# A further pass woven into the expert's own products, in two mixture-of-experts layers on one Trainium2 core

## What is computed

```python
idx = top2 of the best group's scores          # 768 assignments over 16 experts
gates = scores at idx, normalised
for e in range(16):                            # per layer; w1, w3, w2 are 1024 x 1024
    y[e] = (silu(x[e] @ w1[e]) * (x[e] @ w3[e])) @ w2[e]     # x[e]: the tokens of e
out[token] = sum over its two experts of gate * y[e][token]
x = x + g2 * out
```

## Time and profile before

| | us |
|---|---|
| median of 3 runs | 1597.15 (1591.28 to 1598.04) |
| the profiled execution | 1596.13 |
| its span | 1593.1 |
| PE busy in the span | 1482.3 (93%) |
| DVE, ACT busy | 632.8 (40%), 298.3 (19%) |
| read from HBM | 493.06 MB, 310 GB/s over the span |

### The profile page before, as it was taken

How to read it: one execution, slowest core, us unless ns; L and a number is a source line. 1 busy time by engine, 2 the same in 40 slices (tenths; PEclk the granted TensorE clock), 3 DMA queues, 4 the chain that set the end, 5 groups by cost and what they waited for, 6 DMA issues and landing times.

```text
span 1593.1 us, 21276 instructions
## 1 busy us (share of the span) xinstructions
PE 1482.3 (93%) x7798; PEld 719.7 (45%) x7799; DVE 632.8 (40%) x1845; ACT 298.3 (19%) x503; POOL 0.2 (0%) x4
## 2 busy tenths in 40 slices
PE   6999999988899999989999799897999999999996
PEld 3545555645344344434344355454344444344433
DVE  4534666343224332322333548834222333432333
ACT  4422222131010010011010347522101011011001
POOL 0000000000000000000000000000000000000000
PEclk9999999998999999999999899998999999999999
DMA  9448776762969999999987501525699999999992
GB/s 342 178 142 306 262 255 249 313 283 77 391 250 397 425 427 427 425 427 427 424 368 278 196 1 53 211 106 211 285 417 429 424 428 427 403 427 427 424 392 101
DMA packets 67711, 495.29 MB, mean 311 GB/s; under 512 B 4608, under 2 KB 21264, under 8 KB 28368
## 3 DMA queue, kind: packets, MB, share of 16 engines
q1 hardware_dynamic: 66048, 489.33, 75.3%
q10 hardware_dynamic: 1616, 5.33, 1.0%
HBM read 493.06 MB, written 1.58 MB: 310 GB/s over the span
## 4 chain that ended last, share of the span: by engine, by line
PE 78%; DMA 11%; DVE 5%; ACT 3%; issue 2%; ACTq 0%; DVEq 0%; SPq 0%
PE PS L833 76%; DMA halves<-in_moe_w 11%; PE PS L837 2%; DVE xc L1837 1%; ACT hT L575 0%; DVE halves L1658 0%; DVE misc L1658 0%; DVE halves L1651 0%; DVE halves L1649 0%; ACT hT L816 0%; DVE halves L1477 0%; DVE halves L1650 0%; ACT halves L635 0%; ACT halves L736 0%; ACT h L636 0%
## 5 line engine op out<-in xcount | busy, mean ns | idle before, releaser
L833 PE MATMUL PS<-halves,hT 128*64 128x512 f32 x3072 | 674.0, 598 | 17.3 <-DMA halves<-in_moe_w 14.8
L833 PEld LDWEIGHTS PS<-halves,hT 128*64 128x64 f32 x3072 | 218.7, 138 | 454.7 <-issue 429.9
L833 PE MATMUL PS<-hT,halves 128*128 128x384 f32 x640 | 219.7, 499 | 8.4 <-ACT halves L702 6.5
L833 PE MATMUL PS<-halves 128*32 128x512 f32 (+5 forms) x928 | 193.7, 508 | 1.4 <-ACT halves L538 0.7
L833 PEld LDWEIGHTS PS<-hT,halves 128*128 128x128 f32 x640 | 122.2, 194 | 108.0 <-issue 24.3
L1918 DVE COPY misc<-PS 64x512 f32<-64x512 f32 x32 | 21.9, 683 | 335.6 <-PE PS L833 335.6
L833 PEld LDWEIGHTS PS<-halves 128*128 128x128 f32 (+2 forms) x928 | 96.6, 158 | 83.8 <-issue 43.3
L1837 DVE SCALAR_TENSOR_TENSOR xc<-PS,MOD,xc 128x128 f32<-128x128 f32 x336 | 112.3, 409 | 13.8 <-PE PS L833 11.8
L833 PE MATMUL PS<-stack,h 128*128 128x128 f32 x768 | 100.4, 292 | 12.6 <-issue 5.4
L833 PEld LDWEIGHTS PS<-stack,h 128*128 128x128 f32 x768 | 96.0, 206 | 24.0 <-issue 19.8
L597 ACT ACTIVATE hT<-PS 128x512 f32<-128x512 f32 x32 | 19.1, 598 | 433.1 <-PE PS L833 433.1
(11 more groups left out here) (234 smaller groups left out, 978.3 us busy)
## 6 DMA issues: line engine op xcount, KB each, us to landing
halves<-in_moe_w SPq DMA_DIRECT2D x192, 2048.0 KB, 18.2
halves<-in_ada_w SPq DMA_DIRECT2D x48, 1024.0 KB, 6.6
halves<-in_hy_w_in SPq DMA_DIRECT2D x12, 1024.0 KB, 5.1
halves<-in_rg_w_in SPq DMA_DIRECT2D x4, 2048.0 KB, 19.2
halves<-in_hy_w_out SPq DMA_DIRECT2D x4, 1024.0 KB, 9.3
halves<-in_rg_w_out SPq DMA_DIRECT2D x2, 2048.0 KB, 10.5
halves<-in_rg_wa SPq DMA_DIRECT2D x1, 2048.0 KB, 8.4
halves<-in_rg_wx SPq DMA_DIRECT2D x1, 2048.0 KB, 10.9
```

The lines of the kernel that those rows point to most:

```text
L833: return nc.tensor.matmul(out, lhsT, rhs, start=start, stop=stop)
```

## The change

- PE's `extra_pass` is cut into six functions. An expert with `extra > 0` takes a branch of its own in which the first further pass is woven with the base pass: gather, hidden units turned, the pass's tokens turned, w1 and w3 of the pass, **the base w2**, the pass's units turned, (odd experts: both halves of the next tokens), the pass's w2, (odd: the gates), combines. Second and later passes keep an inner loop inside that branch. An expert with `extra < 1` takes a second branch with the old order. The shared parts (units turned, spread, tokens, gates, base w2) so stand twice in the program.
- For an even expert of the branch with a pass, the whole `spread` of the pair before now stands ahead of the pass, and `pass_gather` waits until all eight of its tiles are added (`added(l, group, 8)`, before `8 * r`).
- DVE adds the pass's tiles after it has copied the base output (`pass_added`), and the next expert's base products wait for the pass's tiles in banks 2 and 3. The combine banks are in another order, Xyo and the units' transposition use banks 1 and 7.
- SP: `load_last` now also waits for the pass's w2 (`x_w2_mm`); `freed` waits for `w1_mm` and `w13_mm` of the last user and for its passes, in place of `w13_last`, which is gone.
- PE and DVE read the last expert's counts once more after the loop, and wait for its pass before the layer's last combines.

```diff
-MOE_RELEASE = ("w13_last", "w13_last", "w13_last", "w13_last", "w2_first", "w2_mm")
+MOE_RELEASE = ("w1_mm", "w1_mm", "w13_mm", "w13_mm", "w2_first", "w2_mm")
+X_RELEASE = ("x_w1_mm", "x_w1_mm", "x_w13_mm", "x_w13_mm", "x_w2_mm", "x_w2_mm")
...
                 def load_last(r, e):
+                    passes = passes_to(e - 1)
                     for c in range(4, 6):
-                        load_expert(c, r, e, (MOE_RELEASE[c], NE * l + e))
+                        load_expert(c, r, e, (MOE_RELEASE[c], NE * l + e), (X_RELEASE[c], X_BEGUN + passes))
...
                         for b, at, done_sem in ((2, 0, "w1_mm"), (3, 2, "w13_mm")):
+                            passed(done, b)
                             for k in range(KD):
...
-                        with pe.If(extra > 0):
-                            with pe.Fori(0, extra) as j:
-                                extra_pass(r, group, e, done + j)
...
+                        with pe.If(extra > 0):
+                            if not r:
+                                with pe.If(group > 0):
+                                    spread(l, group, done, 0, 4)
+                                    pe.wait_ge(S("hid"), before("hid", l) + e + 1)
+                                    spread(l, group, done, 4, KD)
+                            pass_gather(r, group, e, done)
+                            units_turned()
+                            pass_tokens(done)
+                            pass_first_two(r, done)
+                            second_matrix()
+                            pass_units(done)
+                            if r:
+                                with pe.If(group < NE // UNROLL - 1):
+                                    pe.wait_ge(S("pick"), before("pick", l) + e + 3)
+                                    tokens_of_two(0)
+                                    tokens_of_two(1)
+                            pass_last(r, done)
+                            if r:
+                                gates_turned()
+                                pe.wait_ge(S("gpT"), before("gpT", l) + group + 1)
+                            pe.wait_ge(S("yo"), GATED + before("yo", l) + e + 1)
+                            pass_combine(done)
+                            with pe.If(extra > 1):
+                                with pe.Fori(1, extra) as j:
+                                    pass_gather(r, group, e, done + j)
...
+                        with pe.If(extra < 1):
...
+                            units_turned()
...
+                            second_matrix()
...
+                extra = pe.value_load(counts_i[0:1, NE - 1:NE], min_val=0, max_val=NX)
+                done = pe.value_load(counts_i[0:1, 2 * NE - 1:2 * NE], min_val=0, max_val=2 * LAYERS * NX)
+                pe.wait_ge(S("x_acc"), X_ADDED + 8 * (done + extra))
...
+                        with dve.If(extra > 0):
+                            pass_added(group, done)
```

More of the change, by code:

```diff
@@ L163, in added, with last_user, freed @@
     return ADDED - 8 + before("acc_done", l) + 8 * pair + tiles
-def freed(l, slot):
-    c = slot % 6
-    return MOE_RELEASE[c], NE * l + (NE - 1 if slot < 4 else NE)
+def last_user(slot):
+    return NE - 2 if slot < 4 else NE - 1
+def freed(l, slot, passes):
+    c, e = slot % 6, last_user(slot)
+    return (MOE_RELEASE[c], NE * l + e + 1), (X_RELEASE[c], X_BEGUN + passes[e])
 ADDED, SPREAD, GATED, X_ADDED, X_BEGUN = 16, 8, 1, 9, 1
@@ L597, in expert_layer, with units_turned, next_tokens @@
                         a.activation(hid, PS[:, 2, :], ACT.Sigmoid).then_inc(S("sig"), 1)
[L598 to L614, removed]
+                        def units_turned():
+                            act.wait_ge(S("hidT_mm"), before("hidT_mm", l) + e + 1)
+                            a.activation(hidT, PS[:, 2, :].rearrange("p (c m) -> p c m", m=P), ACT.Copy) \
+                                .then_inc(S("hidT"), 1)
+                        def next_tokens():
                             with act.If(group < NE // UNROLL - 1):
@@ L1290, in expert_layer @@
                             last.then_inc(S("gpT_mm"), 1)
-                        else:
-                            with pe.If(group > 0):
-                                spread(l, group, done + extra, 4, KD)
-                        passed(done + extra, 6)
-                        pe.wait_ge(S("acc_done"), added(l, group, SPREAD_BANKS.index(6) + 1))
-                        pe.wait_ge(S("hidT"), before("hidT", l) + e + 1)
-                        for k in range(KD):
-                            half = k // 4
-                            if k % 4 == 0:
-                                arrived(4 + half, r, group)
-                            for g in range(2):
-                                last = mm(PS[m * g:m * g + m, 6, :], hidT[:, k % 4, m * half:m * half + m],
-                                          weight(r, 4 + half)[:, k % 4, HALF * g:HALF * g + HALF], k == 0, k == KD - 1)
-                            if k == 3:
-                                last.then_inc(S(MOE_RELEASE[4]), 1)
@@ L1307, in expert_layer, with second_matrix @@
[L1307 to L1312 removed]
+                        def second_matrix():
+                            passed(done, 6)
+                            pe.wait_ge(S("acc_done"), added(l, group, SPREAD_BANKS.index(6) + 1))
+                            pe.wait_ge(S("hidT"), before("hidT", l) + e + 1)
+                            for k in range(KD):
+                                half = k // 4
+                                if k % 4 == 0:
+                                    arrived(4 + half, r, group)
+                                for g in range(2):
+                                    last = mm(PS[m * g:m * g + m, 6, :], hidT[:, k % 4, m * half:m * half + m],
+                                              weight(r, 4 + half)[:, k % 4, HALF * g:HALF * g + HALF], k == 0, k == KD - 1)
+                                if k == 3:
+                                    last.then_inc(S(MOE_RELEASE[4]), 1)
+                            last.then_inc(S("w2_mm"), 1)
```

162 lines of the change are left out of this document (103 added, 59 removed).

## The result

The changed kernel takes **1695.45 us** (median of 4 runs, 1691.29 to 1700.51), the kernel before 1596.27 us: a ratio of 1.0627, 95% interval 1.0605 to 1.0648. The forecast was 1602 us, with a range up to 1668. It is 6.3% slower, and the range missed it. The profiled execution's span is 1695.2 us, 102.1 more than before.

The account below looks back on a forecast made before the run. PE and weight transfers were taken to bound the expert layers in turns. From 1596.1 us, -6.3 (layer 0 weaving), +2.8, +7.0 and +2.0 (missing code blocks, expert 7's gain included) gave 1601.6, median 1602; range 1584 to 1668.

Parts of the forecast that it names:

- The weaving, pass by pass: Five expert passes: new durations from interleaving with base work, worth -6.3 us in layer 0 and -1.5 in layer 1.
- The transfer chain's net gain of 1.0: Layer 0, experts 0 and 2: 8.0 us gained, less jump idle and slow clock, against 3.6 lost to later slots.
- The code's place: PE's expert loop: a pair without a pass touches eight instruction blocks in layer 0, nine in layer 1.
- each number having its place: PE's instruction store: block numbers have fixed places, so 32 and 40 collide, one miss per pair in layer 1.
- C: Rival, chance 0.25: first block in is given up first, nine miss every pair in layer 1; 1647 to 1683 us.
- A missing block costs 1.9 to 3.6 us: PE's jumps to blocks not held: each stop costs this much, read from the earlier trace.
- In layer 0 only expert 14's way back misses: Layer 0, after expert 13's pass: the only missing block there, +1.9 to 3.6 us, taken as +2.8.
- Later misses, under 5.1 per pair, hide behind the transfers: Layer 1 after its first pairs: misses cost nothing, except the one at expert 15, +2.0 us.
- A: The forecast itself, chance 0.33: eight blocks kept in fixed places, about two packets per layer 1 pair, 1602 us.
- B: Rival, chance 0.25: more than eight blocks stay, none is lost, no packets in layer 1; median 1590 us.
- E: Rival, chance 0.10: the weaving itself disappoints, expert 2's later slots costing more than expert 0 saves; 1604 to 1612 us.
- D: Rival, chance 0.07: only neighbouring instruction blocks are kept, so layer 0 suffers as well; about 1725 us.

Follow-up runs that it names:

- straight code, held: Changed kernel without loops for second and later passes, loop head at slot 64 of a block and backward jump announced, 1586.96 us, 0.9954 of the kernel before.
- late-return run: Woven order with TensorE's code written once, head at slot 64, next layer's slots returned at the old time: 1595.71 us, 0.9994 of the kernel before.
- aligned kernel of point 3: Changed kernel without loops for second and later passes, loop head at slot 64 of a block, no announcement: 1596.76 us, 1.0012 of the kernel before.
- old order padded: Kernel before with dead code in each pass branch, giving its loop the changed kernel's block layout: 1697.04 us, 1.0641 times the kernel before.
- kernel without later loops: Changed kernel without its loops for second and later further passes on all three engines, no alignment: 1668.27 us, 1.0487 times the kernel before.

## Why the prediction was wrong

**The weaving, pass by pass: right in its durations.** Forecast and measured (straight code, held): expert 0, 24.4 and 24.7 us (387.82 to 412.50); expert 2, 30.7 and 30.9 (459.29 to 490.22); its first transfer after 13.4 and 13.3 (472.61); expert 13, 30.0 and 30.7; expert 15 to the last combines, 29.6 and 29.4. The transfer chain's net gain of 1.0 (0.8 by its own terms: 8.0 less 1.9 and 1.7 is 4.4, not 4.6) came out as a loss of 0.3, near enough. Costed at nothing and rightly so: the earlier return, by the late-return run. So the order inside each pass was forecast well. The sum was not: -6.3 in layer 0 and -1.5 in layer 1 stand against some -3 in all, because layer 1 as a whole gave +1.7 although expert 7's pass gave its 1.4 (44.6 instead of 46.0 us). In the changed kernel all of it drowned.

**The code's place: right.** The count said eight blocks per ordinary pair in layer 0 and nine in layer 1, and the trace shows exactly this border: none in layer 0's settled pairs, packets in layer 1's, and the sides change when the code moves by 0.19 block. The one exception is layer 0 in the profile of the aligned kernel of point 3, with two packets at eight blocks.

**The failing step** is the sentence that took "eight are kept, each number having its place, so that 32 and 40 push each other out, one miss per pair". By fixed places a pair would fetch two blocks in the old order padded and four in the kernel without later loops; both fetched about nine, as when each block that comes pushes out one that is needed soon. The forecast gave this order, C, a quarter, and its price of a pair (61.3 to 66.4 us) met the 64.9 us of the kernel without later loops. The only argument for a fixed place was that it was "nearest to the rows", but no row told one order from the other: both keep eight, and the old kernel never needed a ninth. This was a choice between 1602 and 1665 with nothing in the trace behind it. Layer 1 was put at +9.0, the pass's gain counted in, and cost 68.2 us in all.

**A second step was mis-sized**: "A missing block costs 1.9 to 3.6 us", from the earlier trace rows. Where no work is queued it was 5.4 us beside transfers, and the smaller stops are best read as what queued products left uncovered. With it fell "In layer 0 only expert 14's way back misses", at +2.8: the way out of the pass of expert 13 misses three times in a row, 16.91 us, and the expert took 16.0 more. The passes of experts 0 and 2 miss too: 21 packets from expert 0 to 4, where the kernel before has five, and 15.0 us more. So layer 0, put at -3.5 in all, cost 34.1 up to layer 1's first expert. Rival C too had "layer 0 ends near zero", which is why its upper end, 1683, lies below the result.

**A third step was wrong even at the forecast's own rate**: "Later misses, under 5.1 per pair, hide behind the transfers". From expert 10 to 15 of layer 1 the changed kernel has about two packets per pair, as in A, and takes 146.4 us instead of 138.8: 7.6 more, where +2.0 was put. PE stops there twice, 8.0 us in all, and never waits for weights. Before, it waited 4.3 us for them in this stretch, and no more than that could be hidden.

B is refuted by the ninth block, E as the cause of the loss by the passes' own times, and D, by which layer 0's pairs suffer as well, by their quiet.

**What would show it:** the text asked for nine packets per pair for C, two for A. The changed kernel has 14 in two middle pairs and two per pair towards the end, so neither number by itself decided. The two layouts with nine blocks in which every pair fetched about nine (old order padded, later loops left out) rule out fixed places.

The Trainium skill, page "Runtime: NRT & Kernel Launch", section "Instruction fetch mechanics", gives TensorE 2048 instructions refilled first in, first out: eight blocks of 16 KiB. The runs agree in the size: settled pairs fetched none at eight, with the one exception above, and always some at nine. On the order they speak for it against fixed places, but not against giving up the block unused for longest, and the two packets per pair at the end of the changed kernel follow from neither as worked out here. The forecast had this rule at hand and gave it less than the fixed places that no page and no row named.

## To carry to other kernels

Count the blocks of 256 instructions that one round of a hot TensorE loop touches, the one behind each jump's landing and behind its end included, and keep them at eight or fewer, rather fewer; a branch that is rarely taken moves everything behind it. Where two rules fit the same silent rows, take the price of both into the choice: dead code in the old kernel would have told them apart at once. And give each aid that a final version uses to the old kernel as well.

## What the runs showed of the hardware

- TensorE keeps eight blocks of 256 instructions (16 KB packets), by these runs. Pairs that touch eight by count fetched none once settled (old kernel, 456 to 900 us; changed kernel, 545 to 810 us), with one exception below. Of those that touch nine, two layouts fetched about nine in each round (18 and 19 packets in two pairs), two others between two and nine. With nine fetched, 7.4 us of a pair were idle, and the granted clock was 0.66 in the 5 us behind one of the stops (1228 to 1233 us).
- A jump into a missing block with nothing queued cost 5.4 us beside transfers at 359 GB/s, 3.3 us at 6 GB/s (three jumps in one stop each), and brought two packets. Stops inside ordinary pairs of the changed kernel's layer 1 are 1.2 to 4.5 us.
- 41 instructions that never run changed the time by 49 us.
- A loop of eight blocks by count had executions of 1591 to 1599 and of 1615 to 1626 us; the profiled one, of the second group, fetched two blocks per pair in layer 0. With the backward jump announced, 12 executions lay between 1583 and 1595 us.
